# An fp32 encoder with routed experts: left half of the down weights in high and low parts, both output halves copied by ScalarE

## The chip, the cores and the metric

The kernel runs on 1 core of one Trainium2 chip. The metric is the time of one execution on the device in microseconds. Line numbers are those of the kernel before the change, as the profile has them, unless a text says otherwise.

## What is computed

Two sequences (512 and 256 tokens, width 1024) go through two layers. Each layer has a mixer (windowed attention and a chunked mLSTM side by side), a cross attention to a memory, and a mixture of experts; behind each stands a layer norm. The part that matters here is the last one. Each of the 768 tokens picks 2 of 16 experts; the tokens of an expert are gathered in blocks of 128, and every block does:

```python
    def expert_block(args):
        xb, e = args
        h = jax.nn.silu(xb @ w_gate[e]) * (xb @ w_up[e])
        return h @ w_down[e]
```

with w_gate and w_up of 1024 x 512 and w_down of 512 x 1024 per expert, all in fp32. The outputs of a token's two experts are scaled by the router's weights and added.

## The kernel before

The engines run one program each and meet at semaphores. The number of expert blocks is known on the chip only: each engine loads it into a register (`n_blocks`), runs `expert_block(b, False)` in a loop `n_blocks - 1` times and then the written-out `expert_block(n_blocks - 1, True)`, for each of the two layers.

**Products in parts.** A weight half lies in one of six slots of 128x2048 fp32 (`expert_part(i)`: 0 and 1 the two halves of the gate weights over k, 2 and 3 left and right up weights, 4 and 5 left and right down weights). For parts 0 to 3 ScalarE copies the raw weights to a rounded high part (`split_part`, L1144; the type fp32r), VectorE subtracts it from the raw ones and leaves the low part in place of the raw weights (`low_part`, L1753). TensorE then forms high x high, high x low and low x high for each k (L2367 for gate, L2377 for up). The tokens of the block are split in the same way (L1177 and L1758). The down weights, parts 4 and 5, are used raw: plain fp32 products of the transposed hidden activations `hbT` (L2403).

**One block on TensorE** (`expert_block` of the tensor program): 24 gate products of 512 columns into bank 2; 24 + 24 up products of 256 columns into banks 3 and 7; two transposes of the left hidden half into bank 4 (L2383); eight transposes of the next block's tokens into banks 0 and 1 (L2348); two transposes of the right hidden half into bank 3 (L2392); four plain products of 512 columns into bank 5 for the left output half and four into bank 6 for the right one (L2403).

**One block on ScalarE**: Silu of the gate products (L1195); copy of the left half of the transposed hidden activations (L1198); high part of the next tokens, two instructions (L1177); copy of the right hidden half (L1205); high part of the next block's part 0; copy of the left output half and its store (L1215, L1217); high parts of parts 1, 2 and 3; store of the right output half (L1230).

**One block on VectorE**: left and right half of Silu times up product (L1853, L1855); low part of the next tokens, two instructions (L1758); low parts of parts 0 and 1; copy of the right output half (L1876); low parts of parts 2 and 3.

SyncE issues the loads of the next block's six weight halves, each when TensorE is through with the slot (L649, L652, L655). GpSimd gathers the tokens of a block ahead (L750) and, beside the first six blocks of a layer, scales x (L774). Behind the loop GpSimd gathers the outputs of the lower expert of each token chunk into the buffers `early` (L780) and then those of the upper one; VectorE adds them to x (L1869, L1890).

TensorE waits before its down products for:

```python
                        pe.wait_ge(moe.yl_ready, b + 1)
                        pe.wait_ge(moe.yr_ready, b + 1)
                        pe.wait_ge(moe.hTl_ready, b + 1)
```

`hTl_ready` and `hT_ready` say that the left and right hidden halves are ready, `yl_ready` and `yr_ready` that the output banks are copied, `dl_loaded` and `dr_loaded` that the down halves are loaded.

## Time and profile before

| | |
|---|---|
| median of 3 runs | 2441.86 us (2433.64 to 2449.81) |
| the profiled execution | 2438.45 us, its span 2436.9 us |
| TensorE busy | 2201.6 us, 90% of the span |
| VectorE busy | 1321.5 us, 54% |
| ScalarE busy | 991.6 us, 41% |
| GpSimd busy | 192.4 us, 8% |
| mean granted TensorE clock | 0.945 of full speed |
| moved by DMA | 385.63 MB, 158 GB/s over the span |

Busy times are sums over the whole program. The expert loops of the two layers fill about 855 to 1165 us and 2022 to 2390 us of the span; the share of an engine there is read from a table of stretches and not from these sums. The chain of waits follows the work that ended last back through whatever released it; its pieces in a stretch say which engine sets the time there.

### The profile page before, as it was taken

How to read it: one execution, taken by the hardware profiler on the slowest of the kernel's cores; microseconds unless marked ns; L12 is line 12 of the kernel's file. 1: busy time of each engine (PE TensorE's matmuls, PEld its weight loads, DVE VectorE, ACT ScalarE, POOL GpSimd, SP SyncE). 2: the span in 40 equal slices, each digit the busy share in tenths (PEclk: the TensorE clock that was granted, in tenths of full speed). 3: DMA queues.
4: the chain of work that ended last, by engine and by line, in shares of the span. 5: the costliest groups of instructions: out<-in, count | busy, mean ns of one | idle time of the engine just before them, and what ended most of it. 6: DMA issues, size and time to landing. Idle time of an engine off the chain costs nothing.

```text
span 2436.9 us, 35264 instructions
## 1 busy us (share of the span) xinstructions
PE 2201.6 (90%) x13226; PEld 1851.5 (76%) x13226; DVE 1321.5 (54%) x2070; ACT 991.6 (41%) x1646; POOL 192.4 (8%) x237
## 2 busy tenths in 40 slices
PE   8699998998988899999698989899898898999992
PEld 7678866988888777777587887598887886777772
DVE  2575367542144666666757636745214456655667
ACT  2355465222231345555235536622324123555552
POOL 0000011000000222000200000100000022200004
PEclk9899988999999899999899999899999989999996
DMA  4711121131200489999511112023210037999995
GB/s 149 281 36 35 38 84 53 53 119 54 87 9 27 169 321 371 380 378 362 196 53 36 36 35 87 26 81 104 70 52 36 27 147 270 373 373 379 381 368 193
DMA packets 78339, 385.63 MB, mean 158 GB/s; under 512 B 10392, under 2 KB 11784, under 8 KB 43400
## 3 DMA queue, kind: packets, MB, share of 16 engines
q1 hardware_dynamic: 55056, 327.83, 35.7%
q0 software_dynamic: 10096, 30.38, 3.5%
q10 hardware_dynamic: 13064, 25.75, 2.8%
q8 instruction: 81, 1.33, 0.2%
q14 instruction: 42, 0.34, 0.0%
HBM read 337.85 MB, written 46.07 MB: 158 GB/s over the span
## 4 chain that ended last, share of the span: by engine, by line
PE 78%; DVE 12%; ACT 5%; issue 3%; DMA 1%; ACTq 0%; DVEq 0%; POOL 0%; SPq 0%; POOLq 0%
PE bank L1959 39%; PE bank L2403 9%; PE bank L2377 8%; PE bank L2367 7%; PE bank L1975 2%; PE bank L2268 2%; PE bank L2097 2%; PE bank L2087 1%; DVE weight_slots_parts L1311 1%; PE bank L2116 1%; PE bank L2348 1%; ACT weight_slots_parts L869 1%; PE bank L2314 1%; DVE weight_slots_parts L1753 1%; DVE mixer_region L1520 1%
## 5 line engine op out<-in xcount | busy, mean ns | idle before, releaser
L1959 PE MATMUL bank<-weight_slots_parts,x_transposed_parts 128*128 128x256 f32 x2496 | 466.9, 289 | 13.9 <-ACT mixer_region L933 13.9
L1959 PEld LDWEIGHTS bank<-weight_slots_parts,x_transposed_parts 128*128 128x128 f32 x2496 | 399.4, 197 | 15.3 <-ACT mixer_region L933 15.1
L1753 DVE TENSOR_TENSOR weight_slots_parts<-weight_slots,mixer_region_parts 128x2048 fp32r<-128x2048 f32 x140 | 324.5, 2337 | 84.7 <-ACT mixer_region_parts L1144 84.5
L1311 DVE TENSOR_TENSOR weight_slots_parts<-weight_slots,weight_slots_parts 128x2048 fp32r<-128x2048 f32 x58 | 132.9, 2292 | 299.0 <-ACT weight_slots_parts L869 298.4
L1959 PE MATMUL bank<-x_transposed_parts,weight_slots_parts 128*128 128x256 f32 (+1 forms) x1024 | 265.4, 347 | 24.0 <-issue 13.0
L1144 ACT ACTIVATE mixer_region_parts<-weight_slots 128x2048 fp32r<-128x2048 f32 x140 | 261.0, 1909 | 23.6 <-ACT x_transposed L1215 18.1
L2403 PE MATMUL bank<-weight_slots,x_transposed 128*128 128x512 f32 x560 | 246.4, 593 | 0.0
L1959 PEld LDWEIGHTS bank<-x_transposed_parts,weight_slots_parts 128*128 128x128 f32 x1024 | 182.5, 195 | 47.9 <-issue 14.4
L2377 PE MATMUL bank<-mixer_region_parts,x_transposed_parts 128*128 128x256 f32 x1120 | 207.8, 284 | 1.5 <-DVE weight_slots_parts L1753 1.4
L2367 PE MATMUL bank<-mixer_region_parts,x_transposed_parts 128*128 128x512 f32 x560 | 195.7, 421 | 7.0 <-DVE x_transposed_parts L1758 7.0
L2403 PEld LDWEIGHTS bank<-weight_slots,x_transposed 128*128 128x128 f32 x560 | 103.4, 190 | 117.9 <-issue 101.7
L2377 PEld LDWEIGHTS bank<-mixer_region_parts,x_transposed_parts 128*128 128x128 f32 x1120 | 176.9, 192 | 5.8 <-DVE weight_slots_parts L1753 4.7
L1959 PE MATMUL bank<-weight_slots_parts,mixer_region_parts 128*128 128x256 f32 x1056 | 176.5, 285 | 4.8 <-DVE mixer_region_parts L1283 4.8
L1959 PE MATMUL bank<-weight_slots_parts,x_parts 128*128 128x256 f32 x576 | 166.0, 288 | 0.0
L2377 PE MATMUL bank<-weight_slots_parts,x_transposed_parts 128*128 128x256 f32 x560 | 158.4, 283 | 0.0
L1959 PEld LDWEIGHTS bank<-weight_slots_parts,mixer_region_parts 128*128 128x128 f32 x1056 | 150.2, 194 | 5.4 <-DVE weight_slots_parts L1311 5.2
L1959 PE MATMUL bank<-mixer_region_parts,weight_slots_parts 128*128 128x512 f32 x512 | 138.4, 391 | 0.0
L2367 PEld LDWEIGHTS bank<-mixer_region_parts,x_transposed_parts 128*128 128x128 f32 x560 | 107.5, 192 | 37.5 <-issue 15.3
L869 ACT ACTIVATE weight_slots_parts<-weight_slots 128x2048 fp32r<-128x2048 f32 x58 | 111.0, 1914 | 56.7 <-DMA weight_slots<-in_wkv_mem 31.2
L1959 PEld LDWEIGHTS bank<-weight_slots_parts,x_parts 128*128 128x128 f32 x576 | 113.7, 197 | 0.0
L1959 PEld LDWEIGHTS bank<-mixer_region_parts,weight_slots_parts 128*128 128x128 f32 x512 | 96.9, 189 | 19.5
L2367 PE MATMUL bank<-weight_slots_parts,x_transposed_parts 128*128 128x512 f32 x280 | 110.9, 396 | 0.0
(284 smaller groups left out, 3585.9 us busy)
## 6 DMA issues: line engine op xcount, KB each, us to landing
weight_slots<-in_w_gate SPq DMA_DIRECT2D x70, 1024.0 KB, 7.2
weight_slots<-in_w_up SPq DMA_DIRECT2D x70, 1024.0 KB, 7.0
weight_slots<-in_w_down SPq DMA_DIRECT2D x70, 1024.0 KB, 7.6
weight_slots<-in_w_in SPq DMA_DIRECT2D x20, 1024.0 KB, 5.1
slots_y<-x_transposed ACTq DMA_DIRECT2D x70, 256.0 KB, 7.2
weight_slots<-in_wkv_mem SPq DMA_DIRECT2D x16, 1024.0 KB, 4.9
slots_y<-mixed SPq DMA_DIRECT2D x2, 6912.0 KB, 33.4
weight_slots<-in_w_out SPq DMA_DIRECT2D x8, 1024.0 KB, 4.9
```

The source lines that it names most:

```text
L869: nc.scalar.activation(half_hi(name), half_raw(name), ACT.Copy).then_inc(w_hi, 1)
L1144: nc.scalar.activation(hi, raw, ACT.Copy).then_inc(moe.high_ready, 1)
L1311: v.tensor_tensor(half_lo(name), half_raw(name), half_hi(name).bitcast(F32), ALU.subtract).then_inc(w_lo, 1)
L1520: ins = v.tensor_tensor(sw_at(g, d, n, sc, lo, hi), bank_of(key)[:, lo * P:hi * P], dec[:, m // 2 % 2, d, 0:(hi - lo) * P], ALU.mult)
L1753: v.tensor_tensor(lo, raw, hi.bitcast(F32), ALU.subtract).then_inc(moe.low_ready, 1)
L1959: ins = pe.matmul(ps, lhs[i](k), rhs[j](k), start=k == 0 and a == 0, stop=k == ks - 1 and a == 2)
L1975: ins = pe.transpose(ps[:, k * P:(k + 1) * P], source(k), ident)
L2097: done(pe.matmul(ps[:, 0:nb * P], qT[hp, j, c * P:(c + 1) * P], kT[hp, k0 * P:(k0 + nb) * P], start=True, stop=True), key)
L2268: ins = pe.matmul(ps[:, jj * 256:(jj + 1) * 256], vm[:, SEQ_OF[2 * cp] * MC + k, j * P:(j + 1) * P], xpt[:, j // 2, k, :], start=(k == 0), ...
L2367: ins = pe.matmul(banks[2][:, :], x_[:, 4 * h + k, :], w_[:, k, :], start=h == 0 and k == 0 and a == 0, stop=h == 1 and k == 3 and a == 2)
L2377: ins = pe.matmul(banks[bank][:, 0:256], x_[:, k, :], w_[:, k, :], start=k == 0 and a == 0, stop=k == KD - 1 and a == 2)
L2403: ins = pe.matmul(banks[5 + h][:, :], hbT[:, k, :], parts[4 + h][0][:, k, :], start=(k == 0), stop=(k == 3))
```

## The change

The left half of the down weights (part 4) is split as the gate and up weights are. ScalarE makes its high part in every block behind the Silu, into a region of its own (columns 2560 to 4608 of the `mixed` buffer), VectorE its low part between the left and the right half of Silu times up. The hidden activations get a high part (`hbT_hi`, by ScalarE) and a low part (`hbT_lo`, by VectorE, `low_hidden`) beside the plain copy, which moves to another buffer; TensorE forms the left output half of 12 products in parts and the right one of 4 plain ones as before. `hTl_ready` and `hT_ready` are now given by VectorE's `low_hidden`. The copy of the right output half goes from VectorE to ScalarE in the loop, as it was in the last block, with its store behind it. The buffers for early gathers become four in place of five, the fourth being the token buffer `xb`, free after the last block's transposes. The semaphores of the constants, the router's weights and its bias become one, as do two of GpSimd's fills.

```diff
@@ -438,7 +439,9 @@
         xbT_lo = xt_parts[:, 4608:5632].rearrange("p (k t) -> p k t", k=KD)
         gact = xt_t[:, 2048:2560]
         hb = xt_t[:, 2560:3072]
-        hbT = xt_t[:, 3072:3584].rearrange("p (k t) -> p k t", k=4)
+        hbT_hi = xt_parts[:, 3072:3584].rearrange("p (k t) -> p k t", k=4)
+        hbT_lo = xt_parts[:, 5632:6144].rearrange("p (k t) -> p k t", k=4)
+        hbT = esc[:, :].rearrange("p (k t) -> p k t", k=4)
         yb = xt_t[:, 3584:4608]
 
         zero_rows = y[:, NC - 1, ATT:D]
...
@@ -467,7 +470,7 @@
         y_ids = y_t[:, NC * D - ATT + 2 * NC:NC * D - ATT + 4 * NC].bitcast(I32)
         tokens = rrow[:, 0:NC * ID_COLS].rearrange("p (c n) -> p c n", c=NC)
 
-        early = [mix[:, 12800:13824], z[:, 2048:3072]] + [y_t[:, 2560 + i * D:2560 + i * D + D] for i in range(3)]
+        early = [mix[:, 12800:13824], z[:, 2048:3072], y_t[:, 4608:5632], xb]
 
         pick = [y_t[:, 2560 + c * P:2560 + c * P + P] for c in range(NC)]
         first_x = y_t[:, 3584:4608]
...
@@ -582,7 +583,8 @@
 
             o = 4096 * slot_of(("wx0", "wx1", "wx2")[i // 2]) + 2048 * (i % 2)
             k = (4, 4, KD, KD, 4, 4)[i]
-            return by_k(ring[:, o:o + 2048], k), by_k(ring_parts[:, o:o + 2048], k), by_k(mix_parts[:, 2048 * i:2048 * i + 2048], k)
+            hi = y_parts[:, 2560:4608] if i == 4 else mix_parts[:, 2048 * min(i, 4):2048 * min(i, 4) + 2048]
+            return by_k(ring[:, o:o + 2048], k), by_k(ring_parts[:, o:o + 2048], k), by_k(hi, k)
 
         def load_half(sp, layer, name):
 
...
@@ -611,8 +613,8 @@
                 load_half(sp, 0, "mk0")
                 sp.dma_start(cst[:, P:C_ALL], consts[:, P:C_ALL]).then_inc(consts_loaded, 16)
                 sp.dma_start(rw_t[:, :].rearrange("p (k e) -> p k e", k=KD),
-                             router_w.rearrange("(k p) e -> p k e", p=P)).then_inc(router_loaded, 16)
-                sp.dma_start(rbias[:, :], router_bias.partition_broadcast(P)).then_inc(router_loaded, 16)
+                             router_w.rearrange("(k p) e -> p k e", p=P)).then_inc(consts_loaded, 16)
+                sp.dma_start(rbias[:, :], router_bias.partition_broadcast(P)).then_inc(consts_loaded, 16)
                 for l in range(DEPTH):
                     now[0] = l
                     moe = experts[l]
...
@@ -787,12 +789,16 @@
                     pool.sem_inc(moe.all_stored, 1)
                     pool.wait_ge(moe.all_stored, 1)
                     for c in range(NC):
+                        if c == len(early) - 1:
+                            pool.wait_ge(moe.xT_filled, 2 * n_blocks)
+                            pool.sem_inc(moe.all_stored, 1)
+                            pool.wait_ge(moe.all_stored, 2)
                         if c >= len(early):
                             pool.wait_ge(combined, 6 * l + c - len(early) + 1)
                         gather_outputs(early[c % len(early)], 0, c, gathered_early[c])
                     pool.wait_ge(moe.y_stored, 32 * n_blocks + 32)
                     pool.sem_inc(moe.all_stored, 1)
-                    pool.wait_ge(moe.all_stored, 2)
+                    pool.wait_ge(moe.all_stored, 3)
                     for c in range(NC):
                         gather_outputs(late(c), 1, c, gathered[c])
 
...
@@ -1183,26 +1191,33 @@
                     act.wait_ge(ids_ready, 1 * l + 1)
                     n_blocks = act.value_load(r_nbi[0:1, 0:1], min_val=NE, max_val=BLOCKS)
 
+                    act.sem_inc(moe.hT_high_ready, 2)
                     act.sem_inc(moe.g_ready, 1)
                     act.sem_inc(moe.yl_ready, 1)
                     act.sem_inc(moe.y_stored, 32)
 
                     by_block = slots_y.rearrange("(b p) d -> b p d", p=P)
+
+                    def hidden(h, bank):
+                        k, a = 2 * h, 256 * h
+                        turned_h = bank[:, a:a + 256].rearrange("p (k t) -> p k t", k=2)
+                        nc.scalar.activation(hbT[:, k:k + 2, :], turned_h, ACT.Copy)
+                        nc.scalar.activation(hbT_hi[:, k:k + 2, :], turned_h, ACT.Copy).then_inc(moe.hT_high_ready, 1)
 
                     def expert_block(b, last):
                         act.wait_ge(moe.h_done, b + 1)
                         act.wait_ge(moe.g_filled, b + 2)
                         nc.scalar.activation(gact, banks[2][:, :], ACT.Silu).then_inc(moe.g_ready, 1)
 
+
+                        split_part(4, moe.dl_loaded, b + 1)
                         act.wait_ge(moe.hTl_filled, b + 1)
-                        nc.scalar.activation(hbT[:, 0:2, :], banks[4][:, 0:256].rearrange("p (k t) -> p k t", k=2), ACT.Copy).then_inc(moe.hTl_ready, 1)
-
+                        hidden(0, banks[4])
                         if not last:
                             act.wait_ge(moe.xT_filled, 2 * b + 4)
                             block_xT()
-
                         act.wait_ge(moe.hT_filled, b + 1)
-                        nc.scalar.activation(hbT[:, 2:4, :], banks[3][:, 256:512].rearrange("p (k t) -> p k t", k=2), ACT.Copy).then_inc(moe.hT_ready, 1)
+                        hidden(1, banks[3])
                         if not last:
                             split_part(0, moe.ga_loaded, b + 2)
                         elif l < DEPTH - 1:
...
@@ -1221,13 +1236,13 @@
                             now[0] = l
                         if not last:
                             split_part(1, moe.gb_loaded, b + 2)
+                        act.wait_ge(moe.y_filled, 2 * b + 3)
+                        nc.scalar.activation(yb[:, 512:D], banks[6][:, :], ACT.Copy).then_inc(moe.yr_ready, 1)
+                        act.wait_ge(moe.yr_ready, b + 2)
+                        act.dma_start(by_block[b, :, 512:D], yb[:, 512:D]).then_inc(moe.y_stored, 16)
+                        if not last:
                             split_part(2, moe.ul_loaded, b + 2)
                             split_part(3, moe.ur_loaded, b + 2)
-                        else:
-                            act.wait_ge(moe.y_filled, 2 * b + 3)
-                            nc.scalar.activation(yb[:, 512:D], banks[6][:, :], ACT.Copy).then_inc(moe.yr_ready, 1)
-                        act.wait_ge(moe.yr_ready, b + 2)
-                        act.dma_start(by_block[b, :, 512:D], yb[:, 512:D]).then_inc(moe.y_stored, 16)
 
                     with act.Fori(0, n_blocks - 1) as b:
                         expert_block(b, False)
...
@@ -1759,7 +1774,7 @@
                                                   xbT_hi[:, 4 * h:4 * h + 4, :].bitcast(F32), ALU.subtract)
                         ins.then_inc(moe.xT_ready, 1)
 
-                    dve.sem_inc(moe.low_ready, 3)
+                    dve.sem_inc(moe.low_ready, 6)
                     dve.sem_inc(moe.h_done, 1)
                     dve.sem_inc(moe.yr_ready, 1)
                     residual_ln(NC + 4, 4, "wx")
...
@@ -1847,17 +1862,28 @@
                         low_weights("kvg")
                         now[0] = l
 
+                    def low_hidden(h, b, signal):
+                        k, a = 2 * h, 256 * h
+                        dve.wait_ge(moe.hT_high_ready, 2 * b + h + 3)
+                        v.tensor_tensor(hbT_lo[:, k:k + 2, :], banks[4 - h][:, a:a + 256].rearrange("p (k t) -> p k t", k=2),
+                                        hbT_hi[:, k:k + 2, :].bitcast(F32), ALU.subtract).then_inc(signal, 1)
+
                     def expert_block(b, last):
                         dve.wait_ge(moe.g_ready, b + 2)
                         dve.wait_ge(moe.ul_filled, b + 1)
                         v.tensor_tensor(hb[:, 0:256], gact[:, 0:256], banks[3][:, 0:256], ALU.mult).then_inc(moe.hl_done, 1)
+                        low_part(4, 5 * b + 5)
                         dve.wait_ge(moe.u_filled, b + 2)
                         v.tensor_tensor(hb[:, 256:512], gact[:, 256:512], banks[7][:, 0:256], ALU.mult).then_inc(moe.h_done, 1)
+                        low_hidden(0, b, moe.hTl_ready)
                         if not last:
                             low_block_xT(b + 1)
-                            low_part(0, 4 * b + 5)
-                            low_part(1, 4 * b + 6)
+                        low_hidden(1, b, moe.hT_ready)
+                        if not last:
+                            low_part(0, 5 * b + 5 + 1)
+                            low_part(1, 5 * b + 5 + 2)
                         else:
+
                             now[0] = l + 1
                             if l < DEPTH - 1:
                                 low_weights("q0")
...
@@ -1871,11 +1897,8 @@
                             now[0] = l
 
                         if not last:
-                            dve.wait_ge(moe.y_stored, 32 * b + 32)
-                            dve.wait_ge(moe.y_filled, 2 * b + 3)
-                            v.tensor_copy(yb[:, 512:D], banks[6][:, :]).then_inc(moe.yr_ready, 1)
-                            low_part(2, 4 * b + 7)
-                            low_part(3, 4 * b + 8)
+                            low_part(2, 5 * b + 8)
+                            low_part(3, 5 * b + 9)
 
                     with dve.Fori(0, n_blocks - 1) as b:
                         expert_block(b, False)
...
@@ -2395,14 +2418,18 @@
                         pe.wait_ge(moe.yl_ready, b + 1)
                         pe.wait_ge(moe.yr_ready, b + 1)
                         pe.wait_ge(moe.hTl_ready, b + 1)
-                        for h in range(2):
-                            pe.wait_ge((moe.dl_loaded, moe.dr_loaded)[h], 16 * b + 16)
-                            for k in range(4):
-                                if h == 0 and k == 2:
-                                    pe.wait_ge(moe.hT_ready, b + 1)
-                                ins = pe.matmul(banks[5 + h][:, :], hbT[:, k, :], parts[4 + h][0][:, k, :],
-                                                start=(k == 0), stop=(k == 3))
-                            ins.then_inc(moe.y_filled, 1)
+                        pe.wait_ge(moe.low_ready, 5 * b + 11)
+                        _, lo, hi = parts[4]
+                        for k in range(4):
+                            if k == 2:
+                                pe.wait_ge(moe.hT_ready, b + 1)
+                            for a, (h_, w_) in enumerate(((hbT_hi, hi), (hbT_hi, lo), (hbT_lo, hi))):
+                                ins = pe.matmul(banks[5][:, :], h_[:, k, :], w_[:, k, :], start=k == 0 and a == 0, stop=k == 3 and a == 2)
+                        ins.then_inc(moe.y_filled, 1)
+                        pe.wait_ge(moe.dr_loaded, 16 * b + 16)
+                        for k in range(4):
+                            ins = pe.matmul(banks[6][:, :], hbT[:, k, :], parts[5][0][:, k, :], start=k == 0, stop=k == 3)
+                        ins.then_inc(moe.y_filled, 1)
 
                     with pe.Fori(0, n_blocks - 1) as b:
                         expert_block(b, False)
```

The instructions of one engine stand in the order in which it runs them. ISA and REGISTER_ALU rows set up a wait. First ScalarE in the loop body, from the Silu (L1195 before, L1210 after) to the copy of the left output half; `x_transposed` holds tokens and hidden activations, `mixer_region_parts` and `mixed_parts` the high parts of weights. Before:

```order
L1195 ACTIVATE x_transposed<-bank2 128x512
L1198 ACTIVATE x_transposed<-bank4 128x256
L1201 ISA
L1177 ACTIVATE x_transposed_parts<-bank0 128x512
L1177 ACTIVATE x_transposed_parts<-bank1 128x512
L1205 ACTIVATE x_transposed<-bank3 128x256
L1143 REGISTER_ALU
L1144 ACTIVATE mixer_region_parts<-weight_slots 128x2048
L1213 ISA
L1214 REGISTER_ALU
L1215 ACTIVATE x_transposed<-bank5 128x512
```

After:

```order
L1210 ACTIVATE x_transposed<-bank2 128x512
L1151 REGISTER_ALU
L1152 ACTIVATE mixed_parts<-weight_slots 128x2048
L1204 ACTIVATE silu_exp<-bank4 128x256
L1205 ACTIVATE x_transposed_parts<-bank4 128x256
L1217 ISA
L1185 ACTIVATE x_transposed_parts<-bank0 128x512
L1185 ACTIVATE x_transposed_parts<-bank1 128x512
L1204 ACTIVATE silu_exp<-bank3 128x256
L1205 ACTIVATE x_transposed_parts<-bank3 128x256
L1151 REGISTER_ALU
L1152 ACTIVATE mixer_region_parts<-weight_slots 128x2048
```

Between the Silu and the left hidden half stands the high part of the down weights, and each hidden half is copied twice. Next the rest of ScalarE's loop body, from the left output copy on. Before:

```order
L1215 ACTIVATE x_transposed<-bank5 128x512
L1217 ISA
L1217 DMA slots_y<-x_transposed 128x512
L1144 ACTIVATE mixer_region_parts<-weight_slots 128x2048 x3
L1230 ISA
L1230 DMA slots_y<-x_transposed 128x512
```

After:

```order
L1230 ACTIVATE x_transposed<-bank5 128x512
L1232 ISA
L1232 DMA slots_y<-x_transposed 128x512
L1152 ACTIVATE mixer_region_parts<-weight_slots 128x2048
L1239 REGISTER_ALU
L1240 ACTIVATE x_transposed<-bank6 128x512
L1242 ISA
L1242 DMA slots_y<-x_transposed 128x512
L1152 ACTIVATE mixer_region_parts<-weight_slots 128x2048 x2
```

The right output copy (bank 6) and its store stand ahead of the last two high parts, those of the up weights. Last VectorE's loop body. Before:

```order
L1853 TENSOR_TENSOR x_transposed<-x_transposed,bank 128x256
L1855 TENSOR_TENSOR x_transposed<-x_transposed,bank 128x256
L1757 ISA
L1758 TENSOR_TENSOR x_transposed_parts<-bank,x_transposed_parts 128x512
L1757 REGISTER_ALU
L1758 TENSOR_TENSOR x_transposed_parts<-bank,x_transposed_parts 128x512
```

After:

```order
L1874 TENSOR_TENSOR x_transposed<-x_transposed,bank 128x256
L1767 ISA
L1768 TENSOR_TENSOR weight_slots_parts<-weight_slots,mixed_parts 128x2048
L1877 TENSOR_TENSOR x_transposed<-x_transposed,bank 128x256
L1867 ISA
L1868 TENSOR_TENSOR x_transposed_parts<-bank,x_transposed_parts 128x256
L1772 ISA
L1773 TENSOR_TENSOR x_transposed_parts<-bank,x_transposed_parts 128x512
L1772 REGISTER_ALU
L1773 TENSOR_TENSOR x_transposed_parts<-bank,x_transposed_parts 128x512
L1867 REGISTER_ALU
L1868 TENSOR_TENSOR x_transposed_parts<-bank,x_transposed_parts 128x256
```

The first piece begins at the left multiply and ends with the low part of the tokens; the low parts of the gate weights, the right output copy (L1876) and the low parts of the up weights follow it. The second begins at the left multiply (L1874 of the kernel after): the low part of the down weights stands between the two multiplies, and a low part of the hidden activations (L1868) on either side of those of the tokens. Behind it follow the four low parts of the next block's gate and up weights with nothing between them.

## Rows read from the trace of the kernel before

**Rows 1.** The page's chain that ended last, and issues of two DMA lines.
```profile
PE 78%; DVE 12%; ACT 5%; issue 3%; DMA 1%; ACTq 0%; DVEq 0%; POOL 0%; SPq 0%; POOLq 0%
...
weight_slots<-in_w_down SPq DMA_DIRECT2D x70, 1024.0 KB, 7.6
...
router_weights<-in_router_w SPq DMA_DIRECT2D x1, 64.0 KB, 19.1
```

**Rows 2.** Stretches of two blocks: us, busy by engine, granted clock, DMA share, GB/s.
```profile
1052.89:1072.30 19.41, 19.41 (x102) 14.61 (x101) 11.72 (x10) 10.26 (x11) 1.53 (x2) 1.00 0.97 371
1072.30:1091.70 19.40, 19.40 (x102) 14.60 (x100) 11.71 (x10) 10.25 (x11) 1.53 (x2) 1.00 0.99 391
```

**Rows 3.** Chain of waits through one block: start us, us, what.
```profile
1053.05 5.47 PE bank L2367 x24
1058.53 5.75 PE bank L2377 x48
1064.28 0.22 PE bank L2383 x2
...
1065.59 6.87 PE bank L2403 x16
1072.46 2.75 PE bank L2367 x12
```

**Rows 4.** Timeline, ScalarE then VectorE: start, us, what [idle before, releaser].
```profile
1064.53 0.38 ACT L1198 ACTIVATE x_transposed<-bank 128x256 f32<-128x256 f32 x1 [5.37 <-PE bank L2383]
1065.41 1.08 ACT L1177 ACTIVATE x_transposed_parts<-bank 128x512 fp32r<-128x512 f32 x2 [0.49 <-PE bank L2348]
1066.38 0.39 ACT L1205 ACTIVATE x_transposed<-bank 128x256 f32<-128x256 f32 x1
1066.64 1.92 ACT L1144 ACTIVATE mixer_region_parts<-weight_slots 128x2048 fp32r<-128x2048 f32 x1
1069.06 0.60 ACT L1215 ACTIVATE x_transposed<-bank 128x512 f32<-128x512 f32 x1 [0.50 <-PE bank L2403]
...
1070.20 5.52 ACT L1144 ACTIVATE mixer_region_parts<-weight_slots 128x2048 fp32r<-128x2048 f32 x3 [0.55 <-ACT x_transposed L1215]
...
1061.44 0.42 DVE L1853 TENSOR_TENSOR x_transposed<-x_transposed,bank 128x256 f32<-128x256 f32 x1 [1.40 <-PE bank L2377]
1064.32 0.42 DVE L1855 TENSOR_TENSOR x_transposed<-x_transposed,bank 128x256 f32<-128x256 f32 x1 [2.46 <-PE bank L2377]
1066.04 1.29 DVE L1758 TENSOR_TENSOR x_transposed_parts<-bank,x_transposed_parts 128x512 fp32r<-128x512 f32 x2 [1.30 <-ACT x_transposed_parts L1177]
1068.59 2.29 DVE L1753 TENSOR_TENSOR weight_slots_parts<-weight_slots,mixer_region_parts 128x2048 fp32r<-128x2048 f32 x1 [1.27 <-ACT mixer_region_parts L1144]
...
1074.36 0.68 DVE L1876 COPY x_transposed<-bank 128x512 f32<-128x512 f32 x1
1074.96 4.49 DVE L1753 TENSOR_TENSOR weight_slots_parts<-weight_slots,mixer_region_parts 128x2048 fp32r<-128x2048 f32 x2
```

**Rows 5.** A block with x scaled beside it: chain, stretch, GpSimd's timeline.
```profile
879.16 3.14 DVE weight_slots_parts L1753
882.30 0.04 issue
882.35 6.02 PE bank L2377 x48
...
869.62:889.68 20.06, 19.71 (x101) 14.45 (x101) 12.68 (x9) 10.47 (x11) 4.45 (x3) 1.00 1.00 394
...
879.07 2.83 POOL L774 TENSOR_SCALAR x<-x 128x1024 f32<-128x1024 f32 x1
```

**Rows 6.** The first block's gate products: chain, and a stretch in them.
```profile
854.59 7.97 PE bank L2367 x24
...
855.00:860.00 5.00, 5.00 (x14) 3.88 (x14) 4.55 (x16) 0.00 (x0) 1.59 (x2) 0.57 0.12 17
```

**Rows 7.** Issues of the down weights' loads, L655, all 70.
```profile
DMA to landing us min/median/max: 4.8/7.6/9.1
```

**Rows 8.** Chain of waits in the last blocks of layer 0 and layer 1.
```profile
1161.34 8.74 DMA weight_slots<-in_w_in
...
2387.45 7.07 PE bank L2403 x16
```

30 lines of the change are left out of this document (15 added, 15 removed).

## The prediction

> **What bounds the kernel now.** I read the page first, for the share of the chain of waits that each engine holds, then the table of stretches for the expert loop, the chain of waits inside one block, and last the timeline of ScalarE and VectorE around it. TensorE holds 78% of the chain [rows 1]. The loads of the down weights come 70 times, two to a block, so the program works 35 expert blocks over the two layers; 33 of them run in the loop body and the last of each layer is written out behind it. In the steady part of the loop every block takes 19.40 us, TensorE is busy for all of it at a granted clock of 1.00, ScalarE for 10.3, VectorE for 11.7, and the DMA engines for 0.97 to 0.99 of the time at 371 to 391 GB/s (the first two of four such stretches in a row, [rows 2]). So TensorE has no gap there, while the transfers are nearly full as well.
>
> The chain of one block [rows 3] is made of TensorE work alone: gate products 5.47 us (24 of 128x512 in parts, 0.228 each), up products 5.75, twelve transposes 1.31 (from 1064.28 to 1065.59), down products 6.87 in 16 passes of 0.429. A plain fp32 product counts two passes, so each half of the output costs 3.435 us.
>
> **What the change removes.** The left half becomes 4 x 3 products in parts, of the shape of the gate products: 12 x 0.228 = 2.735 us in place of 3.435. That is 0.70 us less TensorE work per block, 24.5 us over 35, if TensorE never waits. The VectorE copy of the right output half, 0.68 us, goes; it stood ahead of the low parts of the up weights.
>
> **What it adds beside the path.** ScalarE gets a fourth kind of work per block: the high part of the left down weights (1.92), two extra copies of 128x256 for the high part of the hidden activations (0.38 each) and the right output copy (0.60). VectorE gets one more low part (2.29) and two subtractions of 128x256 (0.42 each, as the multiply of that size [rows 4]). Busy time goes to some 13.5 us on ScalarE and 14.2 on VectorE, well below the block, so neither is full; what counts is where each piece stands in its queue.
>
> **New high part of the down weights.** ScalarE ends the Silu at 0.62 us after the gate products and waited 5.4 us for the transposes ([rows 4], the idle time in front of the row at 1064.53); 1.92 us fit there. VectorE's low part starts behind the left multiply: 1061.44 + 0.34 (a 0.42 us instruction hands over 0.08 before its recorded end, as two low parts of 2.29 take 4.49 together) + 2.29 = 1064.07, and the right multiply starts at 1064.32. It fits with 0.25 us to spare, so I cost it at nothing; if that cover went, the excess would fall on the transposes of the right half. The load of these weights is issued when the left output half is filled, 3.4 us before the gate products and 9.5 us before the Silu ends; loads of down weights land after 7.6 us, at worst 9.1 [rows 7]. Before, they were first needed by the down products, 13 us after the gate products begin. This is enough cover too, but it is the thinnest new one.
>
> **The start of the down products.** TensorE now waits for the low part of the left hidden half. In clock times of the block in [rows 3, 4]: ScalarE's plain copy starts at 1064.53; the next instruction behind a copy of 128x256 starts 0.26 later (1066.38 to 1066.64), so the high part runs from 1064.79 to 1065.17. VectorE starts 0.03 later (the low part at 1068.59 follows a high part that starts at 1066.64 and lasts 1.92) and takes 0.42: 1065.62. TensorE follows 0.05 later, and a product that had to wait costs more than one in the flow: behind such a wait 48 up products took 6.02 us in place of 5.75 [rows 3, 5], 0.27 more. So the down products count from 1065.94 and not from 1065.59: +0.35 us. ScalarE is free again at 1065.1 and the next block's transposed tokens are ready for it at 1065.41 as before, so they don't move.
>
> **The middle of the down products.** Six products take 1.37 us, to 1067.31. The other six want the low part of the right hidden half. Its high part follows the copy at 1066.38 and ends at 1067.02, but VectorE stands in order behind the two low parts of the tokens, which start at 1066.04 and last 1.29; it starts at 1067.26 and ends at 1067.68. With 0.05 and 0.27 the second six count from 1068.00: a wait of 0.69. They end at 1069.37 where the eight passes ended at 1069.02 (1065.59 + 3.435). The 0.70 saved has become +0.35, and the right half, unchanged, ends 0.35 later. This is the term I am surest of: 0.35 + 0.69 = 1.04 of new waits against 0.70.
>
> **The up products of the next block.** ScalarE now copies the right output half before it makes the high parts of the up weights. In [rows 4] the output copy at 1069.06, with its store behind it, lets the next high part start at 1070.20, 1.14 us later, and three high parts in a row take 5.52, a new one each 1.80. Let E be the end of the right half: copy at E + 0.03, high part of the first up half at E + 1.17, VectorE's low part 1.95 later and 2.29 long, so E + 5.41, and TensorE E + 5.46 plus the 0.27 of a restart. The up products want to begin at E + 5.47, when the gate products are through. A wait of about 0.25 us. Before, that high part started at 1072.00, which is E - 0.46 and so 1.6 us earlier; even with VectorE's copy ahead of the low part there was no wait. The bounds here are 0 (the weights' semaphore is just in time and the restart is hidden) and 0.5 (ScalarE behind a second pair of copy and store issue); I take 0.25, to which the rows come nearest.
>
> Per loop block: -0.70 + 0.35 + 0.69 + 0.25 = +0.59, a block of 20.0 us; 33 x 0.59 = +19.5 us. In the first blocks of a layer GpSimd scales x beside VectorE and a low part takes 3.14 in place of 2.29 [rows 5]; there the up products wait already, 20.06 us for the block. The same stretch of GpSimd work would fall on the later low part too, so I let the term stand for them. In the last block of a layer no tokens are turned: the right hidden half is ready in time, the start costs 0.35 against 0.70, and in the first layer a load of the next weights (8.74 us) and the copy behind it, not TensorE, sets the end [rows 8]. 0 to -0.4 us for both, taken as 0. The other edits (waits of the constants on one semaphore, four buffers in place of five for the early gathers, one of them free only after the last transposes) come to 0: the router's weights land 19.1 us after their issue at the very start [rows 1], long before the first tiles that now wait for them, and the early gathers go on beside the last block's down products and stores.
>
> Sum: the profiled execution took 2438.45 us with a span of 2436.9; 2438.45 + 19.5 = 2458. Its time lies 3.4 us under the median of the three runs (2441.86), whose own spread is 16 us, so against the median this is +0.7 to +0.8%, inside the 1% that a measurement of this kernel can tell from no change.
>
> **The rivals.** (1) TensorE's work alone counts. For it: it is what the chain shows in every steady row, and the other engines have 5 us idle. Against: the two hand-overs above are chains of ScalarE and VectorE that end after TensorE gets there. -0.70 x 33 = -23: 2415 us, faster by 1.1%. It would ask for 18.7 us per block; a block moves six loads of 1024 KB, its two output stores of 256 KB and 512 KB of gathered tokens, 7.34 MB, and that would be 393 GB/s, the top of what [rows 2, 5] show (391 and 394), so the transfers may take part of it. The Trainium skill ("DMA: Bandwidth & Descriptors", the table at its head) gives some 358 GB/s from HBM for one core; by that a block could not be under 20.5 us, before the change either, and these stretches at 391 show that it doesn't bind here.
> (2) Restarts are hidden: the 0.27 is the price of a weight load that a wait exposes, and may be smaller in front of 128x512 products; the 16 down passes behind a wait took 7.07 in place of 6.87 [rows 3, 8]. Then start 0.1 to 0.28, middle 0.6, up 0: a block within 0.2 us of before, 2438 to 2444.
> (3) Slower: the new part of the down weights is late. ScalarE holds it in order between Silu and the hidden halves; if its load lands after 9.5 us, or VectorE's low part takes the 3.14 of [rows 5], then the right multiply, the transposes and all behind come 0.4 to 0.6 us later: a block of 20.5, 2438.45 + 33 x 1.1 = 2475, slower by 1.4%. It decides from 0.25 us of delay on VectorE. Against: GpSimd's scaling ends before that place, and 9.1 us is the worst landing.
> (4) The clock. Three short waits per block now cut TensorE's work. The granted clock was 1.00 in the block with a wait at its up products [rows 5], and 0.57 behind the long router stage, where 24 gate products took 7.97 in place of 5.47 [rows 6]. If each block met that once: 33 x 2.5 = 83, 2541 us. The skill ("TensorE: Matmul & The Clock Gate", "A second HAM failure mode") tells of short idle times between groups that make the clock swing; the row with the wait speaks against it.
>
> **How the numbers follow.** Forecast (+0.35 to +0.85 per block, 2450 to 2467) 0.58; rival 1 0.08; rival 2 0.14; rival 3 0.17; rival 4 0.03. Faster by over 1% comes from rival 1 alone: 0.08. Slower by over 1% (above 2466) is rival 3, rival 4 and a tenth of the forecast's upper end with the spread of the runs: 0.28. The rest is 0.64. Range 2436 to 2477: down to rival 2, up over rival 3, with rivals 1 and 4 left out.
>
> **What would show it.** Right: steady blocks of 20.0 us; TensorE's down products of the left half in two groups of six with a wait of 0.6 to 0.7 on VectorE between them and one of 0.3 ahead; the first up product waiting for VectorE's low part; TensorE busy about 1 us less per block than the block is long, clock 1.00; DMA at 367 GB/s. Wrong: blocks under 19.4, or a wait of ScalarE on the down load, or the right multiply starting later than 0.3 us after the right up products end.

## The result and the profile after

| | before | after | ratio, 95% interval |
|---|---|---|---|
| first comparison, median | 2445.24 us (4 runs) | 2471.35 us (4 runs) | 1.0103, 1.0059 to 1.0147 |
| the same kernel again | 2437.78 us (11 runs) | 2467.93 us (5 runs) | 1.0116, 1.0093 to 1.0139 |
| profiled execution, its span | 2438.45, 2436.9 us | 2465.67, 2463.7 us | |

The change makes the kernel 1.0 to 1.2% slower. The forecast was 0.8% slower at 2458 us, inside a range that reached to 2477; the time lies in it. Both measured ratios are just beyond the 1% that I had called the bound of "no change", where most of the chance lay, but both intervals still hold that bound.

The stretch of a steady block, in the columns of [rows 2] (busy time and count for TensorE, its weight loads, VectorE, ScalarE and GpSimd, then clock, DMA share and GB/s):

```profile
1054.43:1074.45 20.02, 19.55 (x105) 15.21 (x105) 14.17 (x12) 13.33 (x14) 1.53 (x2) 1.00 0.98 367
```

A block went from 19.40 to 20.02 us, and TensorE, which had no gap in [rows 2], now has 0.5 us of them. I had expected about 1 us; a first product behind a wait is recorded longer than one in the flow (0.49 in place of 0.39 us), so part of each wait counts as busy. VectorE rose from 11.7 to 14.2 and ScalarE from 10.3 to 13.3, neither near the block. The chain of waits through one block, to be read against [rows 3]:

```profile
1059.91 6.00 PE bank L2400 x48
1065.91 0.22 PE bank L2406 x2
1066.13 0.89 PE bank L2371 x8
...
1067.04 0.61 ACT x_transposed_parts L1185
...
1067.67 0.06 DVE x_transposed_parts L1773
...
1068.28 0.49 DVE x_transposed_parts L1773
...
1068.88 0.42 DVE x_transposed_parts L1868
1069.30 0.04 issue
1069.35 1.67 PE bank L2427 x6
1071.01 3.43 PE bank L2431 x8
1074.45 5.45 PE bank L2390 x24
```

Where [rows 3] had TensorE alone, the chain leaves it at 1067.0 for 2.3 us: ScalarE's high part of the next tokens, VectorE's two low parts of them (L1773), then the low part of the right hidden half (L1868), and only then the second six products in parts (L2427). The up products take 6.00 in place of 5.75. TensorE's weight loads behind these two waits (the bracket is the idle time before and what ended it):

```profile
1067.52 0.19 PEld L2427 LDWEIGHTS bank<-mixed_parts,x_transposed_parts 128*128 128x128 f32 x1 [0.54 <-issue]
...
1069.35 0.19 PEld L2427 LDWEIGHTS bank<-mixed_parts,x_transposed_parts 128*128 128x128 f32 x1 [0.60 <-DVE x_transposed_parts L1868]
```

and what VectorE and ScalarE do at that time:

```profile
1063.41 2.29 DVE L1768 TENSOR_TENSOR weight_slots_parts<-weight_slots,mixed_parts 128x2048 fp32r<-128x2048 f32 x1
1065.95 0.42 DVE L1877 TENSOR_TENSOR x_transposed<-x_transposed,bank 128x256 f32<-128x256 f32 x1 [0.26 <-PE bank L2400]
1066.86 0.42 DVE L1868 TENSOR_TENSOR x_transposed_parts<-bank,x_transposed_parts 128x256 fp32r<-128x256 f32 x1 [0.49 <-ACT x_transposed_parts L1205]
...
1068.88 0.41 DVE L1868 TENSOR_TENSOR x_transposed_parts<-bank,x_transposed_parts 128x256 fp32r<-128x256 f32 x1
...
1074.48 0.60 ACT L1240 ACTIVATE x_transposed<-bank 128x512 f32<-128x512 f32 x1 [0.38 <-PE bank L2431]
1075.63 3.73 ACT L1152 ACTIVATE mixer_region_parts<-weight_slots 128x2048 fp32r<-128x2048 f32 x2 [0.54 <-ACT x_transposed L1240]
...
1077.58 4.49 DVE L1768 TENSOR_TENSOR weight_slots_parts<-weight_slots,mixer_region_parts 128x2048 fp32r<-128x2048 f32 x2 [1.15 <-ACT mixer_region_parts L1152]
```

VectorE ends the first low part of the hidden half at 1067.28 (1066.86 + 0.42), and TensorE's load follows only at 1067.52; the second ends at 1069.29 and the load follows at 1069.35. The right output copy at 1074.48 and its store put the next high part at 1075.63, the low part of the first up half at 1077.58, its end (1077.58 + 2.29) at 1079.87: the up products begin at 1079.93.

**Where the 26.8 us between the two profiled spans are**, by the starts of the first and the last gate products of each layer:

| part of the span | before | after | more |
|---|---|---|---|
| to the first gate products | 854.6 | 851.6 | -3.0 |
| loop of layer 0 (15 periods) | 295.5 | 303.0 | +7.5 |
| end of layer 0 to the gate products of layer 1 | 871.7 | 881.3 | +9.6 |
| loop of layer 1 (18 periods) | 353.5 | 363.5 | +10.0 |
| the last block of layer 1 and the end | 61.6 | 64.4 | +2.8 |

The loops hold 17.5 of it. Part of the rest is at the ends of the layers, where the last store of an output half takes longer than before to land. The last such store of layer 0 and of layer 1 in the chain of waits of the kernel before:

```profile
1172.88 2.12 DMA slots_y<-x_transposed
...
2395.30 2.73 DMA slots_y<-x_transposed
```

and after:

```profile
1177.37 5.16 DMA slots_y<-x_transposed
...
2419.66 4.93 DMA slots_y<-x_transposed
```

That is 3.0 and 2.2 us on the path. The other 6.6 us between the loops fall in code that the change does not touch: 250 us behind the last gate products of layer 0 the kernel after is 2.9 us late, 600 us behind them 9.8. The same instructions between these two points took in the profile before

```profile
1399.50:1749.50 350.00, 323.56 (x2171) 285.64 (x2170) 179.94 (x369) 147.75 (x320) 16.30 (x48) 0.96 0.19 67
```

and in the one after

```profile
1406.90:1763.80 356.90, 330.97 (x2170) 292.28 (x2170) 179.96 (x369) 147.82 (x320) 16.38 (x48) 0.93 0.19 66
```

and in a second profile of the kernel after (changed_again)

```profile
1409.90:1760.30 350.40, 323.61 (x2170) 285.79 (x2170) 179.86 (x369) 147.85 (x320) 16.38 (x48) 0.96 0.19 67
```

The same kernel thus takes 350.4 or 356.9 us for it, with the granted clock at 0.96 or 0.93. From the last gate products of layer 0 to the first of layer 1 the thirteen profiles gave 871.6 to 887.6 us (before 871.7, after 881.3 and again 880.6, copy_on_act 879.6); in changed_again some 5 us of it come only in the last 170 us before the gate products of layer 1. These profiles can't say whether some of that belongs to the change.

### The profile page after: what moved, and what is told of

Its sections match the earlier page's. It is cut to its first block, busy times and chain, and to the rows that moved or that the text cites. A ratio compares the mean times of both kernels' runs of the same rounds, so it can differ in the third digit from the quotient of the medians.

```text
span 2463.7 us, 35869 instructions
## 1 busy us (share of the span) xinstructions
PE 2204.9 (89%) x13366; PEld 1877.1 (76%) x13366; DVE 1402.7 (57%) x2142; ACT 1098.0 (45%) x1784; POOL 199.6 (8%) x237
## 4 chain that ended last, share of the span: by engine, by line
PE 77%; DVE 12%; ACT 6%; issue 3%; DMA 2%; DVEq 0%; ACTq 0%; POOL 0%; SPq 0%; POOLq 0%
PE bank L1982 39%; PE bank L2400 9%; PE bank L2390 7%; PE bank L2431 5%; PE bank L2427 2%; PE bank L1998 2%; PE bank L2291 2%; PE bank L2120 2%; PE bank L2110 1%; DVE weight_slots_parts L1326 1%; PE bank L2139 1%; PE bank L2371 1%; PE bank L2337 1%; ACT weight_slots_parts L875 1%; ACT x_transposed L1016 1%
## 5 line engine op out<-in xcount | busy, mean ns | idle before, releaser
L1768 DVE TENSOR_TENSOR weight_slots_parts<-weight_slots,mixer_region_parts 128x2048 fp32r<-128x2048 f32 x140 | 319.2, 2300 | 122.0 <-ACT mixer_region_parts L1152 121.8
L2431 PE MATMUL bank<-weight_slots,silu_exp 128*128 128x512 f32 x280 | 125.9, 592 | 0.0
L2427 PE MATMUL bank<-mixed_parts,x_transposed_parts 128*128 128x512 f32 x280 | 105.6, 419 | 17.3 <-DVE x_transposed_parts L1868 17.1
L832 ACT ACTIVATE small<-small,constants 128x1 f32<-128x1 f32 (+3 forms) x54 | 16.0, 296 | 232.7 <-DVE small L1584 223.6
L1982 PEld LDWEIGHTS bank<-mixer_region_parts,weight_slots_parts 128*128 128x128 f32 x512 | 96.9, 190 | 19.5
```

The source lines that it names most:

```text
L1768: v.tensor_tensor(lo, raw, hi.bitcast(F32), ALU.subtract).then_inc(moe.low_ready, 1)
L1982: ins = pe.matmul(ps, lhs[i](k), rhs[j](k), start=k == 0 and a == 0, stop=k == ks - 1 and a == 2)
L2427: ins = pe.matmul(banks[5][:, :], h_[:, k, :], w_[:, k, :], start=k == 0 and a == 0, stop=k == 3 and a == 2)
L2431: ins = pe.matmul(banks[6][:, :], hbT[:, k, :], parts[5][0][:, k, :], start=k == 0, stop=k == 3)
```

## The experiments

The theory under test: the change costs the sum of three waits (start and middle of the down products, start of the up products), set by the order of ScalarE's and VectorE's queues, and the saving of 0.70 us per block is really there beneath them. Its rivals: the added work as such (contention, full engines), the buffers for early gathers, or the output store. Below, "block" is a steady block read from the profile, ratio is against the kernel before.

**The output copy alone.** The kernel before with ScalarE's copy of the right half:

```diff
                             split_part(1, moe.gb_loaded, b + 2)
-                            split_part(2, moe.ul_loaded, b + 2)
-                            split_part(3, moe.ur_loaded, b + 2)
-                        else:
...
+                        if not last:
+                            split_part(2, moe.ul_loaded, b + 2)
+                            split_part(3, moe.ur_loaded, b + 2)
...
-                            v.tensor_copy(yb[:, 512:D], banks[6][:, :]).then_inc(moe.yr_ready, 1)
```

> The kernel before with one part of the change: the right output half is copied and stored by ScalarE ahead of the high parts of the up weights, VectorE's copy is gone. Theory (the place in ScalarE's queue costs time): the high part of the left up half starts 1.17 us behind the end of the down products, its low part is ready 5.41 behind it, and the up products start some 0.25 us late: steady blocks of 19.65 us in place of 19.40, about +7 us in all (+0.3%). Rival (the wait for the up weights in the changed kernel needs the two late hidden halves as well, or the freed VectorE pays for it): steady blocks stay at 19.40.

Measured: block 19.67 (+0.27), ratio 1.0030 (0.9999 to 1.0060). The chain of waits has nothing but TensorE, yet its up products are longer than the 5.75 of [rows 3]:

```profile
1051.81 5.25 PE bank L2364 x23
1057.07 5.99 PE bank L2374 x48
```

The timeline has the wait. Here the weight load and the first up product start together, behind VectorE; in the kernel before the load ran 0.22 us ahead of the product (1058.14 and 1058.36):

```profile
1057.05 0.19 PEld L2374 LDWEIGHTS bank<-mixer_region_parts,x_transposed_parts 128*128 128x128 f32 x1 [0.41 <-DVE weight_slots_parts L1753]
1057.05 0.39 PE L2374 MATMUL bank<-mixer_region_parts,x_transposed_parts 128*128 128x256 f32 x1
```

A wait so short that the chain doesn't show it still costs a quarter of a microsecond. The copy by itself is a loss per block, as costed; the interval of the whole time just reaches 1.

**Four early buffers alone**, in the kernel before, with GpSimd's wait for the last transposes that comes with them:

```diff
-        early = [mix[:, 12800:13824], z[:, 2048:3072]] + [y_t[:, 2560 + i * D:2560 + i * D + D] for i in range(3)]
+        early = [mix[:, 12800:13824], z[:, 2048:3072], y_t[:, 4608:5632], xb]
```

> The kernel before with the early gathers in four buffers in place of five, the fourth free after the last transposes; nothing else. Theory (a second gather now waits for VectorE and goes out just ahead of the last output store, which lands behind it): the last store of each layer lands after about 5 us in place of 2.1 and 2.7, the end of each layer is 2 to 3 us longer, +5 us in all (+0.2%); the loop's blocks stay at 19.40. Rival (the 5 us landings of the changed kernel are chance, or come from ScalarE's new work): landings of 2 to 3 us, ends as before.

Measured: block 19.42, ratio 1.0022 (0.9994 to 1.0051). The last store of layer 0, and of layer 1:

```profile
1167.57 4.64 DMA slots_y<-x_transposed
...
2392.90 2.74 DMA slots_y<-x_transposed
```

The slow landing came at layer 0 and not at layer 1: half of what I expected. The whole time is not clear of no change.

**Six early buffers**, in the changed kernel, with one more wait of GpSimd, for the last up products, ahead of gather 4:

```diff
-        early = [mix[:, 12800:13824], z[:, 2048:3072], y_t[:, 4608:5632], xb]
+        early = [mix[:, 12800:13824], z[:, 2048:3072], y_t[:, 4608:5632], xb, xt_t[:, 4608:5632], xt_t[:, 1024:2048]]
```

> The changed kernel with six buffers for the early gathers, the fifth and sixth being the regions of the token parts, free when the last up products are through; no gather waits for VectorE. Theory: all early gathers are issued before the last block's down products end, the last store of each layer lands after 2 to 3 us in place of 5, about -5 us against the changed kernel; blocks stay at 20.02. Rival: landings stay at 5 us since the stores themselves or the order of queues set them.

Measured: block 20.03, ratio 1.0103 (1.0072 to 1.0133), stores 5.23 and 4.48 us. A miss: with six buffers no gather waits for VectorE to free a buffer, but they were still issued from 1164.85 to 1173.60, right ahead of the store at 1175.51. The first of them started 0.8 us after the store of the block before had landed (issued at 1155.96, 8.07 us to land), so they came late as a group.

**The early gathers behind the last store**, in the changed kernel (the wait stands ahead of gather 4 and no longer behind gather 5):

```diff
+                        if c == 4:
+                            pool.wait_ge(moe.y_stored, 32 * n_blocks + 32)
...
                         gather_outputs(early[c % len(early)], 0, c, gathered_early[c])
-                    pool.wait_ge(moe.y_stored, 32 * n_blocks + 32)
```

> The changed kernel with the last two early gathers of a layer issued behind the last output store and not ahead of it. Theory (the last store lands late because gathers issued less than 2.5 us before it are ahead of it in the DMA engines): with the nearest gather about 4 us before the store, it lands after 2 to 3 us at the end of layer 0 in place of 5.2; in layer 1, whose gathers are issued late, 3 to 4. The two gathers then stand ahead of the later ones, so the time as a whole stays within 3 us of the changed kernel. Rival (the store itself is slower beside ScalarE's or TensorE's new work): 5 us as before.

Measured: both stores land in 2.0 us:

```profile
1175.83 2.01 DMA slots_y<-x_transposed
...
2423.36 2.02 DMA slots_y<-x_transposed
2425.37 0.02 issue
...
2426.23 0.94 POOL mixer_region L782
...
2427.47 0.93 POOL scratch L782
...
2428.71 6.08 DMA mixer_region<-slots_y,mixed
```

Block 20.02, ratio 1.0137 (1.0108 to 1.0167), no better than the changed kernel in the same set (1.0116; the median is 4 us higher, where at most 3 were expected). What the store won, two gathers issued in front of the first upper one and its landing of 6.08 (4.55 in after) took again. So the gathers ahead of the store are the cause of its slow landing here, but moving them is no remedy.

Over the thirteen profiles this is a tendency and not a rule. Nine last stores had no gather issued in the 3.7 us before them; they landed in 2.0 to 2.9 us. Seventeen had one within 2.4 us; fifteen of these took 4.1 to 5.7, but one of both_orders (last gather 0.9 ahead) took 3.1 and one of waits_ahead (1.3 ahead) 2.4.

**Both hidden halves ahead of the tokens**, in the changed kernel; on ScalarE and likewise on VectorE:

```diff
                         hidden(0, banks[4])
+                        act.wait_ge(moe.hT_filled, b + 1)
+                        hidden(1, banks[3])
                         if not last:
                             act.wait_ge(moe.xT_filled, 2 * b + 4)
                             block_xT()
-                        act.wait_ge(moe.hT_filled, b + 1)
-                        hidden(1, banks[3])
```

> The changed kernel with both hidden halves ahead of the next block's tokens on ScalarE and on VectorE. Theory (the middle wait is VectorE's order and nothing else): the right low part is ready at about 1.1 us behind the first down product, before the six left-hand products are through (1.37 us less the restart); the middle wait of 0.7 us goes, steady blocks of 19.35 us in place of 20.02, about -22 us against the changed kernel, near -0.1% to +0.2% against the kernel before. The parts of the next tokens come 0.7 us later and still before the gate products need them. Rival (waits of that size sit in the hand-over between engines whatever the order, or the later token parts hold up the gate products): blocks of 19.7 or more.

Measured: block 19.56, ratio 1.0032 (1.0004 to 1.0059). The middle wait is gone, the twelve products run through, and the start is left:

```profile
1055.29 6.01 PE bank L2400 x48
1061.30 0.23 PE bank L2406 x2
...
1061.56 0.39 ACT silu_exp L1204
1061.94 0.28 ACT x_transposed_parts L1205
...
1062.25 0.44 DVE x_transposed_parts L1868
1062.68 0.23 issue
1062.91 3.02 PE bank L2427 x12
```

It gave 0.46 us per block and not the expected 0.67. So the middle wait was worth 0.46 and the start 0.58, and this chain says why: ahead of these products TensorE's queue has four waits in a row and 0.23 us pass between VectorE's end and the weight load, where the middle, with one wait, has 0.04 to 0.06.

**The right output copy behind the first up high part**, in the changed kernel:

```diff
                             split_part(1, moe.gb_loaded, b + 2)
+                            split_part(2, moe.ul_loaded, b + 2)
                         act.wait_ge(moe.y_filled, 2 * b + 3)
...
                         if not last:
-                            split_part(2, moe.ul_loaded, b + 2)
                             split_part(3, moe.ur_loaded, b + 2)
```

> The changed kernel with ScalarE's copy of the right output half behind the high part of the left up half, not ahead of it. Theory: that high part starts 1.6 us earlier, the first up product finds its weights, steady blocks of 19.77 us in place of 20.02 (-0.25), about -8 us against the changed kernel. Rival (three short waits share one slack, so one that goes comes back at the next): blocks of 19.9 to 20.0.

Measured: block 19.74 (-0.28), ratio 1.0073 (1.0047 to 1.0100). The third wait, by itself.

**Both of these orders together.**

> The changed kernel with the two orders of hidden_first and copy_later together. Theory (the waits are separate and add): 20.02 - 0.47 - 0.25 = 19.30 us a block, of which 0.58 is the wait at the start of the down products that is left; about -24 us against the changed kernel and -3 us against the kernel before. Rival (a wait moves to the gate products, whose tokens are split later): 19.5.

Measured: block 19.26 (19.30 expected), ratio 0.9999 (0.9979 to 1.0019). The same work as in the changed kernel, in another order in two queues, gives back all of its loss.

**And three of TensorE's four waits earlier**, ahead of the last two transposes:

```diff
+                        pe.wait_ge(moe.yl_ready, b + 1)
+                        pe.wait_ge(moe.yr_ready, b + 1)
+                        pe.wait_ge(moe.low_ready, 5 * b + 11)
                         pe.wait_ge(moe.h_done, b + 2)
                         for k in range(2, 4):
...
-                        pe.wait_ge(moe.yl_ready, b + 1)
-                        pe.wait_ge(moe.yr_ready, b + 1)
                         pe.wait_ge(moe.hTl_ready, b + 1)
-                        pe.wait_ge(moe.low_ready, 5 * b + 11)
```

> As both_orders, with three of the four semaphore waits that stand before the down products on TensorE (output banks copied, low part of the down weights) moved ahead of the last two transposes; only the wait for the left hidden half stays. Theory (0.23 us pass between VectorE's last write and TensorE's first weight load because its sequencer works through a row of waits and an address step, where 0.05 is the price of one): the start wait falls from 0.58 to about 0.40, blocks of 19.12. Rival (the 0.23 is the price of the hand-over itself): 19.30 as in both_orders.

Measured: block 19.09, ratio 0.9980 (0.9960 to 1.0000). The hand-over falls from 0.23 to 0.04 us, though the semaphores that moved were already up (the latest of them, for the low part of the down weights, 1.6 us before in after):

```profile
1068.91 0.43 DVE x_transposed_parts L1868
1069.35 0.04 issue
1069.39 3.03 PE bank L2427 x12
```

Two of the three stood ahead of the awaited one and one behind it; no run tells which of them costs what.

**Plain products under the hand-overs.** In the changed kernel TensorE forms k = 0 and 1 of the right half first, then the left half in parts, then k = 2 and 3; ScalarE's copies of the output halves each come one high part later:

```diff
+                        pe.wait_ge(moe.hT_high_ready, 2 * b + 3)
+                        pe.wait_ge(moe.dr_loaded, 16 * b + 16)
+                        for k in range(2):
+                            pe.matmul(banks[6][:, :], hbT[:, k, :], parts[5][0][:, k, :], start=k == 0, stop=False)
                         pe.wait_ge(moe.hTl_ready, b + 1)
...
-                        for k in range(4):
-                            ins = pe.matmul(banks[6][:, :], hbT[:, k, :], parts[5][0][:, k, :], start=k == 0, stop=k == 3)
+                        for k in range(2, 4):
+                            ins = pe.matmul(banks[6][:, :], hbT[:, k, :], parts[5][0][:, k, :], start=False, stop=k == 3)
```

> The changed kernel with TensorE's down products in the order: right half k=0,1 (plain, they need ScalarE's copy alone), left half k=0..3 in parts, right half k=2,3; ScalarE's queue suited to it (high parts 0 and 1, left output copy, 2, right output copy, 3). Theory (the loss is hand-overs alone; the saving of 0.70 is real and is seen once something covers them): no wait at the down products nor at the up products, steady blocks of 18.70 us, about -23 us against the kernel before and -1%. Rival (the transfers set the pace: 7.34 MB in 18.70 us is 393 GB/s, the top of what the kernel before moved in one block): blocks of 19.0 to 19.4 with ScalarE waiting for loads of weights.

Measured: block 18.73, ratio 0.9948 (0.9922 to 0.9974). The chain is TensorE alone again, and nearly all of the 0.70 is there (19.40 - 18.73 = 0.67). The time as a whole gained half of the 1% that I expected:

```profile
1054.15 1.72 PE bank L2423 x4
1055.87 2.75 PE bank L2431 x12
1058.62 1.72 PE bank L2434 x4
1060.34 5.48 PE bank L2390 x24
1065.82 5.75 PE bank L2400 x48
```

```profile
1072.00:1091.00 19.00, 19.00 (x109) 15.61 (x107) 14.20 (x12) 13.48 (x16) 1.53 (x2) 1.00 1.01 395
```

VectorE and ScalarE do all the added work here, so that work as such costs nothing. The transfers run at 395 GB/s and still let the block through, which was the doubt about rival 1. The Trainium skill ("DMA: Bandwidth & Descriptors", the table at its head) gives some 358 GB/s as one core's limit from HBM; this row is 10% over it, and the measurement decides.

**The same with the gathers behind the store.**

> The interleaved kernel (blocks of 18.73 us) with those two gathers behind the last store as well. Theory: the store lands after 2 to 3 us in place of 5.2 to 5.4; the whole is within 3 us of the interleaved kernel, 0.5% to 0.9% faster than the kernel before. Rival (the ends of the layers took back 10 of the loop's 22 us because of the gathers): 0.8% to 1.0% faster.

Measured: block 18.73, last stores 2.9 and 2.0 us (5.4 and 5.2 in interleaved), median 2423.21 us, ratio 0.9930 (0.9909 to 0.9952). This is the fastest of all, 0.7% under the kernel before, though its interval overlaps that of interleaved alone.

**The changed kernel again**, in the set of the last two:

> The changed kernel once more, unedited, with more rounds. Theory: 33 loop blocks at +0.62 us (+20.5) less what the first six blocks of a layer already waited before (-3), and +3 to +6 at the ends of the layers: +21 to +24 us, a ratio of 1.009 to 1.010. Rival (half of the 25 us measured at first is the spread between runs): 1.005.

Measured: ratio 1.0116 (1.0093 to 1.0139), block 20.02. The interval leaves out the rival's 1.005 and holds the expected 1.009 to 1.010 at its lower end.

**All of it in one table.** The loop term is 33 times the block's difference from 19.40; measured is the ratio less 1 by the median of the kernel before in that set; the rest is their difference.

| kernel | block | loop term | measured | rest |
|---|---|---|---|---|
| copy_on_act | 19.67 | +8.9 | +7.3 | -1.6 |
| four_buffers | 19.42 | +0.7 | +5.4 | +4.7 |
| changed_again | 20.02 | +20.5 | +28.3 | +7.8 |
| six_buffers | 20.03 | +20.8 | +25.1 | +4.3 |
| gathers_behind | 20.02 | +20.5 | +33.4 | +12.9 |
| copy_later | 19.74 | +11.2 | +17.8 | +6.6 |
| hidden_first | 19.56 | +5.3 | +7.8 | +2.5 |
| both_orders | 19.26 | -4.6 | -0.2 | +4.4 |
| waits_ahead | 19.09 | -10.2 | -4.9 | +5.3 |
| interleaved | 18.73 | -22.1 | -12.7 | +9.4 |
| interleaved_gathers | 18.73 | -22.1 | -17.1 | +5.0 |

Over 43 us the loop term orders the kernels as the times do, but for neighbours closer together than the noise. Each measured value is uncertain by 5 to 8 us, so no single rest says much, but every kernel with other early buffers than the one before has a rest of 2 to 13 us, 6.3 on average, and copy_on_act, which keeps the five, has none. The loop term takes all 33 blocks as steady ones; summed from the profiles the loops differ from the kernel before by +17.5 us in after, +5.3 in copy_on_act, -6.3 in both_orders and -24.8 in interleaved, which makes the rests up to 4 us larger, copy_on_act's 2.0 in place of -1.6. The stores' landings (3.0 + 2.2) are of that size, but where they were cured the rest did not fall for certain (12.9 and 5.0). What makes up the rest beyond them stays open.

## Why the prediction was right, and where not

**The forecast of the block was right, the chance of more than 1% was too low.** A block of 19.99 us was forecast and 20.02 measured; 33 blocks made +19.5 forecast, +20.5 by the steady blocks and +17.5 in the profiled loops. The chance that it was slower by more than 1% stood at 0.28 because the forecast lay 8 us under that line (2466); the some 8 us missed outside the loop carried the measured ratio to it.

**What the change removes.** The 0.70 per block was right: twelve products in parts without a wait take 2.75 us (interleaved), and with all waits covered the block is 0.67 shorter.

**The start of the down products** was undersized: 0.35 forecast, 0.58 measured. Each duration in it held, but "TensorE follows 0.05 later" took the hand-over of a queue with a single wait; behind a row of four it is 0.24, as waits_ahead shows by taking 0.17 us off the block.

**The middle**, the term that I called the surest, was oversized: 0.69 forecast, 0.46 measured. It was reckoned from VectorE's end, and that came as forecast, but the first six products started 0.23 later than I had them and so ended later too; this part of the wait had moved to the start. The sum, 1.04 in both, was right because VectorE's queue sets the end of both.

**The up products**: 0.25 forecast, 0.26 measured (6.01 in place of 5.75), and 0.28 by copy_later, 0.27 by copy_on_act. Nearly all of it is the restart, not the wait.

**The new high part of the down weights** cost nothing, as forecast: in a steady block VectorE's low part ends at 1065.70 (1063.41 + 2.29), 0.25 ahead of the right multiply at 1065.95, just the margin that was worked out. ScalarE never waited for the load, whose worst landing stayed 9.1 us. Rival 3 did not occur.

**The contended first blocks** ("I let the term stand for them") were overcosted. The block that took 20.06 in [rows 5] takes 20.0 in after: there the up products waited for VectorE before the change too, so the saving and the new waits both lie in front of a wait that was there anyway. Hence +17.5 in the loops in place of +20.5.

**The other edits**, costed at 0, are the step that failed. "The early gathers go on beside the last block's down products and stores" was true and was the harm: in the kernel after, where the last was issued 2.4 us or less ahead of the last store, its landing was 3.0 and 2.2 us longer than before, and gathers_behind took this away at both ends. Of some 8 us missed outside the loops this is 5.2; the others stay open. In layer 0 four_buffers shows that the buffer edit does it alone. In layer 1 it does not; there the rows of after show GpSimd slower at issuing, beside VectorE's new low part of the down weights:

```profile
2408.73 2.75 POOL L782 DMA_INDIRECT scratch<-slots_y,mixed  x1 [0.30 <-issue]
...
2417.26 1.90 POOL L782 DMA_INDIRECT scratch<-slots_y,mixed  x1 [0.30 <-issue]
```

The second gather took 0.95 in the kernel before, and the last was issued at 2390.49, 4.8 us ahead of its store; here it is 2.4. What held it up can be read from VectorE's rows of after beside it:

```profile
2408.37 2.28 DVE L1768 TENSOR_TENSOR weight_slots_parts<-weight_slots,mixed_parts 128x2048 fp32r<-128x2048 f32 x1
```

The low part ends at 2410.65 and the gather's issue 0.83 later, at 2411.48. The same holds throughout: of the 312 gathers of outputs in the thirteen profiles 107 took over 1.2 us to issue, and each of these ends 0.81 to 0.85 us behind the end of a VectorE operation with both inputs in SBUF that ran beside it; the rest took 0.93 to 1.16. Beside VectorE operations with an input from a bank alone the issue in after stays at 0.94 or 0.95. VectorE's additions of the gathered outputs hold GpSimd up in this way too, in the kernel before as well. No run moves the low part, so its share in the late last gather (1.8 us) is reckoned from these rows. The Trainium skill ("SBUF — State Buffer", "SBUF: two separate sides") says that a VectorE operation with two inputs in SBUF and a GpSimd one that reads SBUF exclude each other for a whole instruction; the 2.75 beside a low part of 2.28 us fits that.

**The rivals.** Rival 4's time was added up wrongly: 2438.45 + 83 is 2521, not 2541; its chance does not hang on it. Rival 1 needed all waits to vanish and its block of 18.7 came only with another order of the products; even then the gain was 0.5 to 0.7% and not 1.1, since the rest of the program gave some of it back. Rival 2 (restarts hidden) is out: the 0.27 stands in front of products of 256 columns (6.01) and of 512 (3.02 in place of 2.75) alike. Rival 4 is out: the granted clock of the block is 1.00 with three waits in it, as in [rows 2]. The swing that the Trainium skill ("TensorE: Matmul & The Clock Gate", "A second HAM failure mode") tells of for frequent short idle times did not come with these waits.

## What to carry to other kernels

When work is taken from the bounding engine and given to others with time to spare, busy shares do not decide it; the order of their queues does. Work out for each new product when its last input is ready, put the work that the bounding engine waits for ahead of work for later, and keep something for it to do meanwhile: nearly the same instructions gave 1.012 in one order and 0.995 in another. And cost the end of a loop by itself: a few gathers issued just ahead of the last store made it land later, on the path.

## What was unexpected of the hardware

- A row of waits costs time even when all but the last is long fulfilled: 0.23 to 0.24 us from VectorE's end to TensorE's weight load behind four waits, 0.04 to 0.06 behind one (hidden_first against waits_ahead). That is 0.17 us per block.
- A wait of almost no length costs the full restart: the up products took 5.99 to 6.01 in place of 5.75 us where the chain showed no more than 0.03 us between the gate and the up products.
- A store's landing depends on what GpSimd has issued just before: 2.0 to 2.9 us with nothing in the last 3.7 us, mostly 4.1 to 5.7 with a gather in the last 2.4.
- GpSimd's issue of a gather takes 0.94 us alone and up to 2.9 beside a VectorE operation with both inputs in SBUF: it ends 0.81 to 0.85 us behind that operation, all 107 times that it took over 1.2 us.
- The stretch between the two loops, most of it code that no edit touched, took 871.6 to 887.6 us over thirteen profiles, at other granted clocks; differences under some 15 us between two single profiles must be located by stage before they are believed.
